# Moving load order, input projection and last stage of a hybrid trunk kernel, with GpSimd making two low parts

## The reference

```python
h = rms_norm(x, mix_norm);  x = x + mixer_block(h, ...)         # pooling | conv | spatial gating, gated, w_out
h = rms_norm(x, moe_norm);  x = x + moe_ffn(h, ...)             # top 4 of 32 experts
h = rms_norm(x, ple_norm)
x = x + jax.nn.sigmoid(h @ ple_gate_w) * (p @ ple_proj_w)       # 1024x1024 gate, 256x1024 projection
return rms_norm(x, final_norm)
# one expert:
gu = xb @ w_up[e] + b_up[e];  x_glu, x_lin = jnp.split(gu, 2, axis=-1)
x_glu = jnp.minimum(x_glu, 7.0);  x_lin = jnp.clip(x_lin, -7.0, 7.0)
y = (x_glu * jax.nn.sigmoid(1.702 * x_glu) * (x_lin + 1.0)) @ w_down[e] + b_down[e]
```

## Time and profile before

| what | value |
|---|---|
| median of 3 runs | 1192.67 us |
| profiled execution | 1187.05 us |
| its span | 1185.3 us |
| PE busy in the span | 1115.4 us (94%) |
| VectorE, ScalarE, GpSimd busy | 441.0, 241.5, 10.5 us |
| moved by DMA | 447.52 MB, 378 GB/s over the span |
| mean granted TensorE clock | 0.988 |

### The profile page before, as it was taken

How to read it: one execution, slowest core, us unless ns; L and a number is a source line. 1 busy time by engine, 2 the same in 40 slices (tenths; PEclk the granted TensorE clock), 3 DMA queues, 4 the chain that set the end, 5 groups by cost and what they waited for, 6 DMA issues and landing times.

```text
span 1185.3 us, 14625 instructions
## 1 busy us (share of the span) xinstructions
PE 1115.4 (94%) x5831; PEld 534.1 (45%) x5831; DVE 441.0 (37%) x718; ACT 241.5 (20%) x323; POOL 10.5 (1%) x29
## 2 busy tenths in 40 slices
PE   8999999899999999999999999999999999999975
PEld 8999998433333333333333333333333333333335
DVE  5999895723322222222222222222222222222054
ACT  5455453211111111111111111111111111111154
POOL 2000000000000000000000000000000000000000
PEclk9999999999999999999999999999999999999998
DMA  9864569999999999999999999999999999999930
GB/s 307 301 209 157 189 249 321 371 414 430 424 431 427 430 429 428 430 426 430 427 430 428 430 429 428 429 427 399 429 429 429 428 430 427 430 426 430 424 156 35
DMA packets 58408, 447.52 MB, mean 378 GB/s; under 512 B 4115, under 2 KB 26891, under 8 KB 33707
## 3 DMA queue, kind: packets, MB, share of 16 engines
q1 hardware_dynamic: 57236, 443.65, 90.6%
q0 software_dynamic: 672, 1.99, 0.5%
q10 hardware_dynamic: 471, 1.47, 0.4%
HBM read 446.05 MB, written 1.05 MB: 377 GB/s over the span
## 4 chain that ended last, share of the span: by engine, by line
PE 50%; DMA 37%; DVE 8%; ACT 3%; issue 1%; SPq 1%; DVEq 0%; ACTq 0%
DMA down_ring<-in_expert_w_down_dram 27%; PE ps L1616 16%; PE ps L1657 15%; DMA up_ring<-in_expert_w_up_dram 9%; PE ps L1439 6%; PE ps L1449 3%; PE ps L1670 1%; DVE work L1264 1%; PE ps L1523 1%; PE ps L1753 1%; DVE w_lo L421 1%; DVE work L1260 1%; PE ps L1647 1%; DVE work L1256 1%; ACT hT L797 1%
## 5 line engine op out<-in xcount | busy, mean ns | idle before, releaser
L1616 PE MATMUL ps<-up_ring,hT 128*64 128x512 f32 x2048 | 447.8, 593 | 8.1 <-DMA up_ring<-in_expert_w_up_dram 7.2
L1616 PEld LDWEIGHTS ps<-up_ring,hT 128*64 128x64 f32 x2048 | 153.3, 137 | 296.1 <-issue 279.8
L1657 PE MATMUL ps<-down_ring,hT 128*64 128x512 f32 x1024 | 243.6, 619 | 30.9 <-DMA down_ring<-in_expert_w_down_dram 24.5
L1256 DVE TENSOR_SCALAR work<-ps 128x512 f32<-128x512 f32 x32 | 22.1, 691 | 505.8 <-PE ps L1629 505.8
L1657 PEld LDWEIGHTS ps<-down_ring,hT 128*64 128x64 f32 x1024 | 72.2, 141 | 178.3 <-issue 150.5
L1239 DVE TENSOR_TENSOR x_sb<-x_sb,ps 128x1024 f32<-128x1024 f32 x64 | 77.7, 1214 | 169.0 <-PE ps L1670 163.6
L792 ACT ACTIVATE work<-work 128x512 f32<-128x512 f32 x32 | 20.2, 630 | 439.7 <-DVE work L1256 439.6
L640 ACT ACTIVATE w_hi<-up_ring 128x2048 fp32r<-128x2048 f32 x31 | 59.2, 1914 | 78.4 <-PE ps L1449 42.1
L1439 PE MATMUL ps<-h_hi,w_hi 128*128 128x256 f32 x304 | 74.2, 284 | 0.0
L1439 PE MATMUL ps<-h_lo,w_hi 128*128 128x256 f32 x304 | 73.7, 283 | 0.0
L421 DVE TENSOR_TENSOR w_lo<-up_ring,w_hi 128x2048 fp32r<-128x2048 f32 x32 | 72.9, 2283 | 2.0 <-ACT w_hi L640 1.0
(11 more groups left out here) (252 smaller groups left out, 822.9 us busy)
## 6 DMA issues: line engine op xcount, KB each, us to landing
up_ring<-in_expert_w_up_dram SPq DMA_DIRECT2D x128, 2048.0 KB, 26.9
down_ring<-in_expert_w_down_dram SPq DMA_DIRECT2D x64, 2048.0 KB, 21.8
up_ring<-in_w_in_dram SPq DMA_DIRECT2D x21, 1024.0 KB, 5.4
up_ring<-in_branch_w_dram SPq DMA_DIRECT2D x6, 1024.0 KB, 5.2
up_ring<-in_w_out_dram SPq DMA_DIRECT2D x4, 1024.0 KB, 6.0
up_ring<-in_ple_gate_w_dram SPq DMA_DIRECT2D x4, 1024.0 KB, 27.0
x_sb<-in_x_dram SPq DMA_DIRECT2D x2, 512.0 KB, 3.9
up_ring<-in_w_in_dram SPq DMA_DIRECT2D x2, 512.0 KB, 6.3
```

The lines of the kernel that those rows point to most:

```text
L1256: nc.vector.tensor_scalar(glu, ps[:, GLU, :], LIMIT, None, ALU.min).then_inc(glu_ready, 1)
L1616: last = nc.tensor.matmul(ps[64 * g:64 * g + 64, GLU + part, :], xe[:, j, k % 4, k // 4, :], w[:, D * part + 512 * g:D * part + 512 * (g + ...
L1657: last = nc.tensor.matmul(ps[64 * g:64 * g + 64, Y, :], actT[:, r, c, :], down_units[:, c, D * r + 512 * g:D * r + 512 * (g + 1)], start=( ...
```

## The change

It has six parts.

1. *Load order.* The change to the order up(q), down(q) comes at expert 16 instead of 22, and at it the loads of up(17) and down(16) are interleaved. The projection weights are loaded before up(16). The last up unit of expert 31 is loaded as two 1 MB rows with a semaphore each.
2. *Projection.* Its four quarters are now one quarter of the columns each, for both halves of the tokens, done in front of the last up unit of experts 26 to 29. The result lies in `b_rest`, over the weights already used.
3. *Last expert.* `to_tokens(30, 0)` stands in front of the last up unit; the product, its transposes and copies are made in two halves; `to_tokens(30, 1)` stands before `down(31)`, whose two halves now follow each other; the copy of y is VectorE's.
4. *Start of the last stage.* The transposes of x stand behind the jump, one half of the tokens at a time. VectorE makes h_hi and h_lo of the first half, ScalarE h_hi of the second, in pieces of 128 columns with a semaphore count for each. The first gate matmuls need the first half only. PSUM banks and the order of the gate products change with this.
5. *Low parts.* GpSimd makes `w_lo` of gate units 0 and 1; VectorE makes those of 2 and 3.
6. *Last sigmoids.* ScalarE does `gate_sigmoid(2)`, `(3)` and `(4)` one step earlier each.

The diff, cut to its core:

```diff
-FINAL_BANK = [4, 5, 6, 7, 1]
-EARLY_LOADS = 22
+FINAL_BANK = [6, 7, 4, 5, 0]
+EARLY_LOADS = 16
+PROJ_FIRST, PROJ_PARTS = 26, 4
...
+            e = EARLY_LOADS
+            refill_up(e, 0, e)
+            refill_down(e - 1, e - 1)
+            for c in range(DOWN_UNITS):
+                refill_up(e + 1, 1, e + 1, [c])
+                refill_down(e, e, [c])
+            refill_up(e + 1, 1, e + 1, range(DOWN_UNITS, UP_UNITS))
+            refill_down(e + 1, e + 1)
...
+            for m in range(2):
+                pool.wait_ge(g_hi_ready, m + 1)
+                gate_lo_part(nc.gpsimd, m).then_inc(g_lo_ready[m], 1)
...
-            split_gate(1)
-            split_gate(2)
+            for m in range(4):
+                split_gate(m)
             act.wait_ge(x_final, 1)
             act.dma_start(final_gain, on_all(final_norm)).then_inc(gain_loaded, 16)
-            act.wait_ge(xsT_done, 3)
-            scale_high(0, ROW["ple_norm"], h_hi)
-            split_gate(3)
+            act.wait_ge(xfT_done, 2)
+            for k in range(KT):
+                gain = ROW["ple_norm"] + k
+                nc.scalar.activation(h_hi[:, k, P:2 * P], final_columns(1, k), ACT.Copy,
+                                     scale=prm[:, gain:gain + 1]).then_inc(xf_hi_ready[1], 1)
...
             tile_squares(0)
+            gate_sigmoid(2)
             tile_squares(1)
             nc.scalar.activation(small[:, 34:35], eps, ACT.Sigmoid)
-            gate_sigmoid(2)
+            gate_sigmoid(3)
             tile_squares(2)
-            gate_sigmoid(3)
+            gate_sigmoid(4)
             tile_squares(3)
-            gate_sigmoid(4)
...
+            def last_expert(q, e):
+                expert_weights(q, e)
+                add_result(q - 1, 0)
+                gated_product(q)
+                for h in range(2):
+                    rows = slice(2 * h, 2 * h + 2)
+                    nc.vector.tensor_tensor(act_cols[:, :, rows],
...
+                                            ALU.mult).then_inc(act_half_ready, 1)
+                add_result(q - 1, 1)
+                dve.wait_ge(down_used, DOWN_UNITS * (q + 1))
+                nc.vector.tensor_copy(y_sb, ps[:, Y, :]).then_inc(y_ready, 1)
...
+            dve.wait_ge(xfT_done, 1)
+            for k in range(KT):
+                gain = ROW["ple_norm"] + k
+                nc.vector.tensor_scalar(h_hi[:, k, 0:P], final_columns(0, k), prm[:, gain:gain + 1], None,
+                                        ALU.mult).then_inc(xf_hi_ready[0], 1)
+            final_low_parts(0)
+            for m in range(2, 4):
                 split_gate(m)
             dve.wait_ge(rms_ready, 2)
             nc.vector.reciprocal(rstd, rms).then_inc(rstd_ready, 1)
-            for m in range(2, 4):
-                split_gate(m)
+            final_low_parts(1)
...
+                    if c == UP_UNITS - 1 and part is not None:
+                        ple_projection(part)
+                    if c == UP_UNITS - 1 and early_result:
+                        to_tokens(q - 1, 0)
...
-            hT_written(3)
+            transpose_final(0)
...
+            gate_pass((0, 1), g_hi, h_hi, range(0, 6))
+            transpose_final(1)
+            gate_pass((0, 1), g_hi, h_lo, range(0, 6))
+            gate_pass((0, 1), g_hi, h_hi, range(6, KT))
+            gate_pass((0, 1), g_hi, h_lo, range(6, KT))
             gate_pass((2,), g_hi, h_hi)
-            gate_pass((2,), g_hi, h_lo)
+            gate_pass((3,), g_hi, h_hi)
             gate_pass((0, 1), w_lo, h_hi)
```

More of the change, by code:

```diff
@@ L1249, in expert, with gated_product @@
                 make_weight(q)
[L1250 to L1253 removed]
+            def gated_product(q):
                 dve.wait_ge(up_done, q + 1)
```

244 lines of the change are left out of this document (153 added, 91 removed).

## The result

The changed kernel takes 1177.61 us (median of 4 runs, 1176.54 to 1178.25) against 1192.66 (4 runs, 1188.74 to 1195.56) for the kernel before. The ratio is 0.9875, with a 95% interval of 0.9846 to 0.9904: faster by 15 us, between 11 and 18. The forecast was 1179.

The account below looks back on a forecast made before the run. The weight queue bounds the experts, then a chain over engines bounds the end. Steps A to G sum to -13.45, taking the profiled 1187.05 us to 1173.6; the median's 5.6 offset makes it 1179, range 1169 to 1188.

Parts of the forecast that it names:

- A: Last up unit of expert 31: it starts as its weights land, so its bias starts at 1121.7, -5.3 us.
- B: Bias end to down in the last expert: only half the product, transposes and copy stand in front, -1.0 us.
- C: Last expert's down to the copy of y: two halves at 3.65 us, -2.7; a falling clock would return 1.7.
- D: Copy of y to first transpose: the 4.26 us jump over unused code now stands before the transposes, +1.9 us.
- E: First transpose to first gate product: only half the transposes and one piece of h_hi in front, -4.05 us.
- F: First gate product to tile 0's sigmoid: half-width products and the other transposes added, low parts hidden, +0.2 us.
- G: Tile 0's sigmoid to the end: ScalarE's third sigmoid precedes the table loads, others one step earlier, -2.5 us.
- R2: Rival: the jump grows while gate loads fill the queue, +2, and the clock falls in down, +1.7; median 1183; chance 0.14.
- R1: Rival: lock-out or slow start on GpSimd delays the w_lo products by 1 to 6 us; median 1182; chance 0.12.
- R4: Rival: GpSimd's low parts near their upper bound, 31.6 us each, giving 1222 as a median; chance 0.02.
- R3: Rival: the jump is short or hidden and the load gap vanishes, -2 and -2; median 1175; chance 0.10.
- R5: Rival: the order change at expert 16 opens several gaps, the queue losing over 10 us; about 1190; chance 0.05.

Follow-up runs that it names:

- e7: The kernel before with only the projection moved to experts 26 to 29: 1184.79 us, ratio 0.9935.
- e4: The changed kernel with the load order of before, the last unit still as two rows: 1176.65 us, ratio 0.9867.
- e5: The changed kernel with two up units of the next expert loaded ahead of the down units for experts 17 to 20: 1174.8 us, ratio 0.9861.
- e11: The changed kernel with 24 dummy transposes issued between the last `to_tokens` and the jump: 1179.93 us, ratio 0.9915.
- e9: The kernel before once more, with no edit, for a second trace: 1192.35 us, span 1190.6.
- e1: The changed kernel again, with no edit, as a yardstick: 1180.76 us, ratio 0.9894.
- e2: The changed kernel with TensorE's last stage inside both branches, so the jump comes after the last gate product: 1176.07 us, ratio 0.9853.
- e6: The changed kernel with the edits of e5 and e2 together: 1173.69 us, ratio 0.9842.
- e12: The changed kernel with the edits of e6 and all four low parts on VectorE: 1172.05 us, ratio 0.9840.
- e10: The changed kernel with low parts exchanged, VectorE making units 0 and 1, GpSimd 2 and 3: 1185.35 us, one run.
- e3: The changed kernel with all four low parts on VectorE, none on GpSimd: 1178.22 us, ratio 0.9874.
- e8: The kernel before with TensorE's last stage inside both branches, so the jump comes last: 1186.22 us, ratio 0.9950.

## Why the prediction was right, and where its steps were not

The time (1179 forecast, 1177.61 measured), the sign and the range held. The sum inside it did so only in part, and that the time is so close is luck: two errors, in the sum and in the offset put on it, cancelled. Profile against profile:

| step | from, to | predicted | measured | ends at, in the changed kernel |
|---|---|---|---|---|
| A | last unit's bias starts | -5.3 | -4.6 | 1122.46 |
| B | bias to down | -1.0 | -0.8 | 1126.84 |
| C | down to the copy of y | -2.7 | -2.9 | 1133.97 |
| D | copy of y to first transpose | +1.9 | +3.45 | 1140.61 |
| E | first transpose to first gate product | -4.05 | -3.1 | 1143.03 |
| F | first gate product to first sigmoid | +0.2 | +1.6 | 1159.28 |
| G | from there to the end | -2.5 | -2.7 | the span ends at 1176.4 |
| sum | | -13.45 | -8.9 | |

- **A held.** TensorE no longer comes late. It waits for the unit before the last, which landed at 1114.12, where step A had it at 1113.2, and is busy from there to the bias: 3.65, then `to_tokens`, then 3.58. The 0.7 that is missing is that later landing. The last rows (issued at 1080.1, 38.9 to land) were there at 1119.1, just behind the 1118.88 at which their unit began with its first half, so their own semaphore saved 0.2 us at most. e7 shows the same step alone, 5.2 us against its landings. That was the largest term; by the medians of e7 the projection's move is about half of the gain.
- **B and C held in this trace.** The `to_tokens` in front and the single piece of down gave 7.10 us at a granted clock of 1.00, with nothing between its halves. e7 shows that without them the slow half (5.35 us) stays. But in three of the ten profiles with this form (e4, e5, e11) down took 8.67 to 8.79 us, so the 1.7 us that the prediction had set aside for a falling clock did come back in them. C is the usual case, not a sure one.
- **D was mis-sized.** The step was seen, with its place and sign: the jump is exposed since the transposes are behind it. But the 4.26 us of the earlier trace rows were taken as the jump's duration, and here it took 5.82. Other executions had 4.84 (e9), 4.13 (e1), 3.74 (e5) and 3.35 (e2). One row of a single record was not a constant.
- **E and F failed, by one cause that D set off.** Both were costed at full clock. The 3.91 us of idle time in D let the clock fall to 0.50; the eight transposes cost 1.98 instead of 1.07, and the first twelve gate products 4.53 instead of 3.0. This is rival R2's mechanism, the jump that grows and the clock that falls, but here it struck behind the jump and not in down, where R2 had put it. e2 takes the jump away and the 0.9, the 1.5 and the idle time go together, and e6 and e12 repeat it, so that the exposed jump is the cause is shown. That it acts through the idle time is what the granted clock says; e11 fits it, without deciding it. In e4 and e5 the clock stayed up, and TensorE still stood idle for 0.70 and 0.76 us behind the tenth gate product, for nothing that the profile shows; with the jump last that pause is not there.
- **G held**: the third sigmoid stands before the table loads (1163.14, the first load at 1164.45). Before, ScalarE then stood idle for 1.55 and 0.95 us until VectorE had the next tiles of x; now their squares follow without a wait, and 0.56 in front of the third sigmoid is the last idle piece. No run has this part alone.
- **The load term** was 0, with a range of -2 to +0.3. The gap is now 3.0 us instead of 2.0, so about +1, beyond the bad end; in e1 and e10 the new order cost 4 us (see e4). In this pair of profiles it doesn't show in the last landing: that is 0.8 later, and the mixer's last weights were 0.9 later already. e5 shows that the gap wasn't bound to be there.
- **GpSimd held**, with room to spare: 4.5 us each where 5 was taken, done at 1142.5 for products that begin at 1155.6. The page "GPSIMD Engine Reference" of the Trainium skill (3.1, side-by-side cycle accounting) has 4497 ns for a `tensor_tensor` of 2048 float32 columns (there an addition, here a subtraction), and the trace agrees with 4504 and 4542 ns. VectorE was later than forecast (units 2 and 3 done at 1151.2 and not 1148, the second h_lo at 1158.3), but TensorE asked for that h_lo only at 1159.25. R1 and R4 did not occur; e3 shows that even the benefit is nil. R3's jump was not short, and R5's loss of queue time was about 1 us and not 10.
- **The offset hid the error.** To the profiled sum 5.6 us were added, since the median of before lies that much above its profiled execution. e9 shows what these were: mostly low clock that this one execution had escaped, above all the stall behind the jump. In the changed kernel's profiled run the stall occurred, and its median is 0.6 below that run, not 5.6 above. So the sum gave too much by 4.6 (1173.6 for 1178.25) and the offset too much by 6.2, in the other direction. Against a typical execution of before (e9: 1190.6 of span) the change saves 14.2, close to the 13.45 of the steps and the 15 of the medians. That closeness is luck as well: which steps would be on the slow clock was not foreseen for either kernel.

A small misreading in the prediction changed nothing: it gives the DMA rate as up to 434 GB/s, and the highest value in the earlier trace rows is 431.

Open is why the jump's length varies between 3.3 and 5.8 us. R2's reason, that it grows while the gate loads fill the queue, is not borne out. With these loads under way it took 3.62 to 5.82 us (e4, e5, e3, e1, e10, the change). With the queue empty it took 3.35 to 3.90 at the very end (e2, e8, e6, e12) and 3.33 in e11, but 4.26, 4.66 and 4.84 in the old kernel form (the first trace, e7, e9). No experiment held the one fixed and varied the other. Parts 3, 4 and 6 of the change were never run alone, either; what they are worth is read from the steps of one pair of profiles.

## What to carry to other kernels

A jump over unused code costs microseconds on the engine's sequencer: put it where the engine has nothing left to do, and when work is moved, ask which instructions now stand behind a jump that used to stand in front of it. An idle time of TensorE can have a second price, the clock of the products after it, so a stall is to be costed with the products behind it, once at each of the two clock levels. Before adding the distance between a profiled execution and the median to a forecast, find out what in the profile makes it: a second trace of the same kernel is enough.

## What the runs showed of the hardware that was not expected

- **The taken jump** on TensorE's sequencer took 3.3 to 5.8 us in the records of different executions of nearly the same code (4.26 and 4.84 in the kernel before itself). In the change it began with the eight `to_tokens` products queued ahead of it; with 24 transposes queued behind these it began 2.6 us later (e11).
- **The clock** is not a function of the idle time just ahead: 3.36 us of it left the clock at 1.00 in the first trace of before, and 1.28 to 1.83 did so in e4, e5, e8 and e11; 3.76 to 3.94 us let it fall to 0.50 (e7, e9 and the change), but so did 2.97 in e10 and 2.2 in e1 and e3 (1.69 and 1.54 us for the eight transposes, 1.09 at full clock). The down product of the last expert, with the same products and the same idle pieces of 1.49 and 0.23 us ahead, ran in 7.09 us in seven profiles of the changed form and in 8.67 to 8.79 in e4, e5 and e11. The stretch of it in e5:

```profile
1124.00:1134.00 10.00, 9.54 (x36) 3.23 (x36) 1.55 (x3) 4.76 (x5) 2.42 (x1) 0.83 1.00 399
```

The granted clock is 0.83 there, where the change had 1.00. So 1.7 us of difference between executions come from this stage alone.

- **A gap in the weight queue** costs TensorE nothing where it occurs and shows at the end: TensorE was busy for 15.00 of 15 us around the gap at 705 us, and without it e5's last landing still came 1.9 us earlier.
- **VectorE's `w_lo`**, an instruction with two SBUF inputs, nearly stands still while GpSimd's is under way: 3941 ns instead of 2281, and no cost on GpSimd (4.52 and 4.57 us). Its instructions with one input from PSUM don't: in the change the two adds to x (1135.89 to 1138.24) ran beside GpSimd's and took 1.22 and 1.21 us, as they did in e3, where GpSimd was idle.
